# Joined inverses of two token tiles: turning four blocks of both tiles by one 128x128 transpose, with masks, sums and copies over two neighbouring banks

## The reference, cut to what matters

```python
A = jnp.where(strict, bc[..., :, None] * kk * decay, 0.0) + jnp.eye(C, dtype=jnp.float32)
u = lax.linalg.triangular_solve(A, bc[..., None] * vc, left_side=True, lower=True, unit_diagonal=True)
w = lax.linalg.triangular_solve(A, bc[..., None] * jnp.exp(G)[..., None] * kc,
                                left_side=True, lower=True, unit_diagonal=True)
```

```python
def step(state, inp):
    r_t, w_t, k_t, v_t, a_t, b_t = inp
    sa = jnp.einsum("bhvk,bhk->bhv", state, a_t)
    state = state * w_t[:, :, None, :] + sa[..., None] * b_t[:, :, None, :] + v_t[..., None] * k_t[:, :, None, :]
    return state, jnp.einsum("bhvk,bhk->bhv", state, r_t)
```

## Time and profile before

| | |
|---|---|
| three runs | 2663.7, 2663.72, 2672.25 us; median 2663.72 |
| profiled execution | 2665.42 us, its span 2663.6 us |
| PE matmuls | 2478.5 us busy (93%), 15332 |
| PE weight loads | 2084.5 us (78%), 15332 |
| DVE | 1805.8 us (68%), 2484 |
| ACT | 1426.0 us (54%), 1924 |
| POOL | 323.0 us (12%), 215 |
| mean granted TensorE clock | 0.948 |

### The profile page before, as it was taken

How to read it: one execution, slowest core, us unless ns; L and a number is a source line. 1 busy time by engine, 2 the same in 40 slices (tenths; PEclk the granted TensorE clock), 3 DMA queues, 4 the chain that set the end, 5 groups by cost and what they waited for, 6 DMA issues and landing times. The chain is left out here.

```text
span 2663.6 us, 40356 instructions
## 1 busy us (share of the span) xinstructions
PE 2478.5 (93%) x15332; PEld 2084.5 (78%) x15332; DVE 1805.8 (68%) x2484; ACT 1426.0 (54%) x1924; POOL 323.0 (12%) x215
## 2 busy tenths in 40 slices
PE   7878989998998999989998997799999999999998
PEld 6457658988886699866997986688888888888887
DVE  3665445557665555573455764788898888998897
ACT  4242234445553444243444642578777777778776
POOL 4110200004542000000002531000000000000000
PEclk9888799999999999988998999899999999999999
DMA  6510125543322255522554400899999999999995
GB/s 252 172 56 10 69 72 177 189 171 134 137 92 99 99 171 180 182 87 95 190 182 163 147 33 1 325 369 386 381 369 377 391 366 387 378 377 376 380 381 217
DMA packets 180012, 573.88 MB, mean 215 GB/s; under 512 B 11966, under 2 KB 81726, under 8 KB 136764
## 3 DMA queue, kind: packets, MB, share of 16 engines
q1 hardware_dynamic: 175932, 558.27, 56.3%
q0 software_dynamic: 2992, 11.01, 1.6%
q10 hardware_dynamic: 976, 3.03, 0.3%
HBM read 564.16 MB, written 6.29 MB: 214 GB/s over the span
## 5 line engine op out<-in xcount | busy, mean ns | idle before, releaser
L3637 DVE TENSOR_TENSOR moe_weights_low<-ring,moe_weights_high 128x1024 fp32r<-128x1024 f32 x672 | 779.8, 1218 | 95.5 <-ACT moe_weights_high L3886 95.4
L3886 ACT CAST moe_weights_high<-ring 128x1024 fp32r<-128x1024 f32 x672 | 687.0, 1053 | 108.9 <-PE banks L258 106.1
L256 PE MATMUL banks<-moe_weights_high,moe_rows_high 128*128 128x512 f32 x896 | 354.6, 396 | 3.1 <-DVE moe_rows_low L3642 2.5
L258 PE MATMUL banks<-moe_weights_low,moe_rows_high 128*128 128x512 f32 x896 | 350.2, 391 | 0.0
L257 PE MATMUL banks<-moe_weights_high,moe_rows_low 128*128 128x512 f32 x896 | 349.5, 390 | 0.0
L256 PE MATMUL banks<-ffn_x_high,ffn_weights_high 128*128 128x256 f32 x1056 | 299.1, 283 | 0.7 <-DVE ffn_x_low L3260 0.7
L257 PE MATMUL banks<-ffn_x_high,ring_low 128*128 128x256 f32 x1056 | 297.5, 282 | 0.0
L258 PE MATMUL banks<-ffn_x_low,ffn_weights_high 128*128 128x256 f32 x1056 | 297.4, 282 | 0.0
L3436 DVE TENSOR_TENSOR ring_low<-ring,ffn_weights_high 128x2048 fp32r<-128x2048 f32 x60 | 134.8, 2288 | 128.6 <-ACT ffn_weights_high L3410 128.6
L256 PEld LDWEIGHTS banks<-ffn_x_high,ffn_weights_high 128*128 128x128 f32 x1056 | 199.1, 189 | 4.2 <-DVE ffn_x_low L3260 1.4
L257 PEld LDWEIGHTS banks<-ffn_x_high,ring_low 128*128 128x128 f32 x1056 | 199.5, 189 | 2.7
(11 more groups left out here) (630 smaller groups left out, 4744.4 us busy)
## 6 DMA issues: line engine op xcount, KB each, us to landing
ring<-in_moe_gate_pieces SPq DMA_DIRECT2D x112, 1024.0 KB, 7.0
ring<-in_moe_up_pieces SPq DMA_DIRECT2D x112, 1024.0 KB, 7.2
ring<-in_moe_down_pieces SPq DMA_DIRECT2D x112, 1024.0 KB, 7.2
ring<-in_ffn_w SPq DMA_DIRECT2D x66, 1024.0 KB, 7.8
ring<-in_od_w_in SPq DMA_DIRECT2D x10, 2048.0 KB, 8.0
ring<-in_o_w_in SPq DMA_DIRECT2D x8, 2048.0 KB, 9.2
ring<-in_e_ffn_w_gate SPq DMA_DIRECT2D x11, 1024.0 KB, 5.4
ring<-in_e_ffn_w_up SPq DMA_DIRECT2D x11, 1024.0 KB, 8.0
```

Of the source, the lines that this page charges most:

```text
L256: pe.matmul(out_, lh, rh, start=start, stop=False)
L258: return pe.matmul(out_, lh, rl, start=False, stop=stop)
L3637: dve.tensor_tensor(lo[:, b], piece, hi[:, b].bitcast(F32), ALU.subtract).then_inc(sems["lo_done"], 1)
L3886: act.copy(hi[:, b * 1024:(b + 1) * 1024], piece).then_inc(sems["hi_done"], 1)
```

## The change

The two tiles of a pair now share one tile each for `blocks`, `blocks_t` and `low`. `blocks` is 128x512 with the columns ordered by head, tile, column, so that the 128 columns of one head hold both tiles' blocks side by side. T becomes one 128x128 transpose for each head (four a pair, into one bank), which puts the tile on the partitions and the side into the columns; one ACT copy of 128x512 takes it to `blocks_t`. P1 and P2 keep 16 products of 64x64: P1 writes with the tile on the partitions and one bank for each side, P2 takes tile on the partitions as input and writes side on the partitions, one bank for each tile. The mask, the sum and the first copy become single operations over two neighbouring banks, which a new helper `take_two` takes from an even number on, passing over a bank where the turn is odd. P1 and T of a pair are written in one go, each with its own semaphore count. `start_blocks` and `finish_inverse` read and write the new layout. An older function, `invert`, which nothing called, is removed.

```diff
+        def take_two():
+            if turn[0] % 2:
+                turn[0] += 1
+            at = turn[0] % BANKS
+            both_banks = psum[:, at * BANK:(at + 2) * BANK].rearrange("p (s n) -> p s n", s=2)[:, :, 0:256]
+            return [take_bank(), take_bank()], both_banks.rearrange("p s (j n) -> p s j n", j=4)
...
+                pair["by_tile"] = pair["blocks"].rearrange("p (j t n) -> p t j n", t=TT, n=64)
...
-                    for g, bank in zip(pair, two):
-                        act.copy(g["blocks"], bank.ap[:, 0:256]).then_inc(*S.tick())
+                    act.copy(pair["by_tile"], together).then_inc(*S.tick())
...
-                    two = [take_bank() for _ in pair]
+                    two, together = take_two()
+                    bank = take_bank()
...
                         for j in range(4):
-                            for g, bank in zip(pair, two):
-                                for b in sides:
-                                    last = pe.matmul(bank.ap[across(g, b), col(j)], g["NT"][b, j, b], g["blocks"][b, col(j)],
+                            for t, g in enumerate(pair["groups"]):
+                                for b, of_side in zip(sides, two):
+                                    last = pe.matmul(of_side.ap[sides[t], col(j)], g["NT"][b, j, b], pair["by_tile"][b, t, j, :],
                                                      start=True, stop=True)
                         last.then_inc(*M.tick())
-                    have = M.at()
+                        for due in unseen(pe, bank.free):
+                            pe.wait_ge(*due)
+                        for j in range(4):
+                            last = pe.transpose(bank.ap[:, j * P:(j + 1) * P], pair["blocks"][:, j * P:(j + 1) * P], ident)
+                        last.then_inc(*M.tick())
+                    turned = M.at()
+                    have = turned[0], turned[1] - 1
...
-                        for g, bank in zip(pair, two):
-                            dve.tensor_tensor(r4(g["low"]), r4(bank.ap[:, 0:256]), wide(const(f"level{s}")), ALU.mult).then_inc(*V.tick())
+                        dve.tensor_tensor(pair["low"].rearrange("p (j b n) -> p b j n", b=2, n=64), together,
+                                          const(f"level{s}").unsqueeze(1).unsqueeze(1).to_broadcast([P, 2, 4, 64]),
+                                          ALU.mult).then_inc(*V.tick())
...
-                        for j in range(4):
-                            for g, bank in zip(pair, two):
-                                for b in sides:
-                                    last = pe.matmul(bank.ap[across(g, b), col(j)], g["blocks"][b, col(j)], ident[b, b],
-                                                     start=True, stop=True)
...
-                        for g, bank in zip(pair, two):
-                            act.copy(g["blocks_t"], bank.ap[:, 0:256]).then_inc(*S.tick())
+                        act.copy(pair["blocks_t"], bank.ap.rearrange("p (s n) -> p s n", s=2)).then_inc(*S.tick())
...
                         for j in range(4):
-                            for g, bank in zip(pair, two):
-                                for b in sides:
-                                    there = across(g, b)
-                                    last = pe.matmul(bank.ap[b, col(j)], g["blocks_t"][there, col(j)], g["low"][there, col(j)],
+                            for t, of_tile in enumerate(two):
+                                for n_side, b in enumerate(sides):
+                                    at = 2 * j + n_side
+                                    last = pe.matmul(of_tile.ap[b, col(j)], pair["blocks_t"][sides[t], at // 4, col(at % 4)],
+                                                     pair["low"][sides[t], col(at)], start=True, stop=True)
...
-                        for g, bank in zip(pair, two):
-                            dve.tensor_tensor(g["blocks"], g["blocks"], bank.ap[:, 0:256], ALU.add).then_inc(*V.tick())
+                        dve.tensor_tensor(pair["by_tile"], pair["by_tile"], together, ALU.add).then_inc(*V.tick())
```

More of the change, by code:

```diff
@@ L1371, in _ @@
                         act.wait_ge(*turned)
-                        for g, bank in zip(pair, two):
-                            act.copy(g["blocks_t"], bank.ap[:, 0:256]).then_inc(*S.tick())
-                    for g, bank in zip(pair, two):
-                        bank.free = g["turned"] = S.at()
-                for n_pair, pair in enumerate(pairs):
-                    two = [take_bank() for _ in pair]
+                        act.copy(pair["blocks_t"], bank.ap.rearrange("p (s n) -> p s n", s=2)).then_inc(*S.tick())
@@ L1389, in _ @@
                         last.then_inc(*M.tick())
-                    have = M.at()
+                    have = pair["last_product"] = M.at()
                     @block.vector
                     def _(dve):
-                        for due in unseen(dve, [g["have"] for g in pair]):
+                        for due in unseen(dve, pair["have"]):
                             dve.wait_ge(*due)
                         dve.wait_ge(*have)
-                        for g, bank in zip(pair, two):
-                            dve.tensor_tensor(g["blocks"], g["blocks"], bank.ap[:, 0:256], ALU.add).then_inc(*V.tick())
@@ L1411, in _ @@
                 def _(pe):
-                    for due in unseen(pe, bank.free, bank2.free, g["have"]):
+                    for due in unseen(pe, bank.free, bank2.free, pair["have"]):
                         pe.wait_ge(*due)
                     for j in range(4):
-                        last = pe.matmul(bank2.ap[lower, col(j)], g["NT"][upper, j, lower], g["blocks"][upper, col(j)], start=True, stop=True)
+                        last = pe.matmul(bank2.ap[lower, col(j)], g["NT"][upper, j, lower], blocks[upper, j, :], start=True, stop=True)
                     last.then_inc(*M.tick())
@@ L1418, in _ @@
                         for b in sides:
-                            last = pe.matmul(bank.ap[b, col(j)], g["blocks"][b, col(j)], ident[b, b], start=True, stop=True)
+                            last = pe.matmul(bank.ap[b, col(j)], blocks[b, j, :], ident[b, b], start=True, stop=True)
                     last.then_inc(*M.tick())
@@ L1437, in finish_inverse @@
                 bank.free = g["turned"] = S.at()
-            for g in groups:
+            for pair in pairs:
+                g = pair["groups"][t]
+                low = pair["low"][:, t * 256:(t + 1) * 256]
                 bank = take_bank()
@@ L1445, in _ @@
                     for j in range(4):
-                        last = pe.matmul(bank.ap[upper, col(j)], g["low"][lower, col(j)], r4(g["XT"])[lower, j, lower], start=True, stop=True)
+                        last = pe.matmul(bank.ap[upper, col(j)], low[lower, col(j)], r4(g["XT"])[lower, j, lower], start=True, stop=True)
                     last.then_inc(*M.tick())
@@ L4708, in deltanet @@
             clear([*first, *second])
-            finish_inverse(first)
+            finish_inverse(pairs, 0)
             for w in first:
                 solve(w)
-            finish_inverse(second)
+            finish_inverse(pairs, 1)
             for w, w2 in zip(first, second):
```

222 lines of the change are left out of this document (36 added, 186 removed).

## The result

| | before | after |
|---|---|---|
| median, runs (lowest to highest) | 2663.70 us, 11 runs (2657.06 to 2672.25) | 2643.63 us, 11 runs (2641.31 to 2659.93) |
| a second set of runs | 2661.4 us, 23 runs (2653.08 to 2669.73) | 2643.73 us, 6 runs (2639.99 to 2653.02) |
| ratio of the times, 95% interval | | 0.9933 [0.9916, 0.995]; second set 0.9933 [0.9909, 0.9958] |
| profiled execution, span, granted clock | 2665.42, 2663.6, 0.948 | 2650.51, 2648.7, 0.952 |
| the same, a second profile | 2657.35, 2655.5, 0.953 | 2652.4, 2650.6, 0.95 |

The change makes the kernel faster, by 0.7% (0.4 to 0.9% by the two intervals). I had forecast 2652.8 us with a range that ended at 2646. The direction, the mechanism and the length of a level were right; the gain I gave was too small and the range too narrow.

The account below looks back on a forecast made before the run. TensorE's instruction fetch, 256 per 3.6 us, was taken to pace the inverses. Gains of 4.5 and 5.2 us there plus 1.2 in the finish, 10.9 together, took 2665.42 to 2654.5, or 2652.8 us as median; range 2646 to 2662.

Parts of the forecast that it names:

- The level: One of five levels of each inverse: 4.00 us by its path, 3.87 by the fetch, where it took 5.2.
- pair step: First product plus turn of one pair in a level: 1.20 us instead of 1.01, including 0.15 for the shape change.
- the way behind P2: From a level's second product to the next level: 1.66 us less 0.06 for the merged sum.
- The one stall: Fetch block arriving 0.4 us late at the first turn of the last level.
- the mask and the copy are covered: Within a level, mask ready at 1.57 us and copy of T at 1.90, before the second pair step ends at 2.40.
- The finish: Fetch stalls opening the finish of both inverses, 0.5 and 0.7 us, would go: 1.2 us gained.
- From the profiled execution to the median: Whole-run time: profiled forecast 2654.5 us, median taken 1.7 lower, 2652.8; 3 us added on either side for run spread.
- The first: Rival on the inverse's levels: the fetch keeps hold, 4.5 us a level, 2657.4 us on the median's scale; chance 0.14.
- the fourth: Rival on the inverse's levels: shape changes overlap with work, fetch paces levels at 3.87 us, median 2650.8 us; chance 0.10.
- The second: Rival on the inverse's stalls: not from instruction count, so they stay; levels 0.30 us longer, median 2666.7 us; chance 0.05.
- The third: Rival on TensorE's clock in the inverses: lower level granted, levels of 6.2 us, 2676.5 us; chance 0.05.
- The fifth: Rival on both stages: something beside the inverse sets their end, no change, median 2663.7 us; chance 0.04.

Follow-up runs that it names:

- e2: Changed kernel with merged masks, sums and copies kept, but the turn again by sixteen 64x64 products; 2658.9 us, 11 runs, ratio 0.9994 to the kernel before.
- e8: Changed kernel plus 14 idle small products (2 weight columns) per pair and level, 387 instructions a level as before the change; 2660.63 us, one run.
- e7: Changed kernel plus 35 small idle products (140 instructions) ahead of the first turn of mix0's inverse; first run 2640.84 us.
- e10: The same kernel as e7, timed: changed kernel plus 35 idle products ahead of mix0's first turn; 2644.3 us, ratio 0.9932 to the kernel before.

## Why the prediction was wrong, step by step

**What bounds the kernel: right.** Instructions arrived 256 at a time and paced the levels; e2 keeps the pace with the narrow turn, e8 brings it back by the count, and e7 moves the boundary.

**The level: right.** 4.00 us forecast; mix0's first products start at 218.52, 222.56, 226.57, 230.70 and 234.70, so 4.04, 4.01, 4.13 and 4.00. The pair step was 1.26 instead of 1.20 (0.20 between P1 and T where I had taken 0.15), and the way behind P2 1.57 instead of 1.60. The one stall stood at the turn that I had named and took 0.6 us and, in the second profile, 0.3, against 0.4. That the mask and the copy are covered held as well. In gdn the levels took 4.07, 4.36, 4.33 and 3.99 us, in the second profile 4.07, 4.36, 4.01 and 4.00. I had looked for one late block in each inverse; in gdn there was one in the second level and, in the first profile, another in the third. The second level took 4.36 us in e7 as well, whose block ended there without a pause; that one has a second cause, which stays open.

**The gain of the two inverses: right.** 9.7 us forecast. By the table the mean is 25.24 to 20.87 in mix0 and 26.11 to 21.06 in gdn, 4.4 + 5.0 = 9.4. It is the mean over two profiles that fits; the first pair alone gives 3.8 + 4.5.

**The finish: mis-sized.** I gave 1.2 us for two stalls that open it. From its first product to its last weight load it took 10.64, 9.43, 9.68 and 10.75 us before (mix0, gdn, then the second profile) and 8.38 or 8.44 after: 10.1 to 8.4, so 3.4 us for the two. The two without the lower clock (9.43, 9.68) give 1.0 and 1.3 each, twice what I took; the other two ran 5.0 and 3.4 us at the lower level. With the inverses this is 9.4 + 3.4 = 12.8; the remaining 0.4 of the 13.3 us lies in the first turn, which in one profile of after was spared the lower level. So the sum should have been 13.3 instead of 10.9.

**From the profiled execution to the median: this is the step that failed.** I took the median to lie 1.7 us below the profiled time, as it had in three runs, and allowed 3 us for the clock. Of the miss of 9.2 us, 6.8 lie here:
- 2.4 us are not of this step but of the finish and the first turn above.
- 2.8 us are the three runs of before: over 89 runs in five sets its median is 2660.9, not 2663.7.
- 4.0 us are left. The medians lie 2660.9 - 2643.6 = 17.3 apart, the stages 13.3. The runs of the kernel after fall into 13 from 2640.0 to 2647.0 us at mean granted clocks of 0.951 to 0.957, and 4 from 2650.5 to 2659.9 us at 0.948 to 0.952. Both profiled executions are among the four, so the traces show the rarer case, and the median leaves it out. The means, 2661.0 and 2645.8, lie 15.2 apart, with a standard error of 1.4.

So 13.3 us are accounted for in the traces. The rest of the kernel, the span less the two stages, shows what else moves the time: it took 2588.0 and 2577.7 us in the profiles of before, 2585.6 and 2586.7 in those of after, 2577.5 in e7 and 2576.8 in e10, where 262, 236, 256, 264, 235 and 233 us of it ran at the lower level. TensorE has the same instructions in it (the idle products of e7 and e10 apart), and its "issue" waits there were 9.6 to 10.9 us in all six. The kernel before reached a rest as short as e7's to 0.2 us, so no trace shows one that is shorter by the change. Whether the 2 to 4 us beyond the stages belong to the change (a lower level granted less often somewhere behind it) or to the chance of 17 runs is open; the wider interval of the ratio, 11 to 24 us, holds both.

**The rivals.** The first (4.5 a level) and the fourth (3.87, the change of shape for nothing) are both excluded by levels of 3.99 to 4.36, 4.10 on average. The second (stalls not from the number of instructions) is excluded by e7 and e8. The third looked for the lower clock inside the inverse; it was granted 1.00 there in both profiles, and it was the old inverse that ran 3.4 us of each at the lower level in both profiles. I had seen that on the earlier trace rows and weighed it only as a risk, not as something that could be gained back. The fifth is excluded by the result.

## What to carry to other kernels

Count the instructions of a small-tile loop, not only its products: where "issue" waits stand at equal distances in the count, one wide operation in place of many small ones paid here even though it is slower on the array, and making DVE and ACT lighter paid nothing until that was done. A wait of TensorE at such a place may be put down to another engine whose work had long ended. A gain read from one pair of profiles holds for the stage that was changed; before a difference elsewhere is put down to the change, profile the old kernel a second time. Where the granted clock differs by several thousandths from run to run, the range of a forecast has to be as wide as that makes it, whatever the sum says.

## What the runs showed of the hardware

- In these two loops TensorE got its instructions in blocks of 256, one in 3.58 to 4.10 us (e8), and paused up to 1.6 us at a boundary (before), in the middle of a group of like products.
- 140 idle instructions put into a wait ahead of mix0's inverse removed its last stall (0.6 us) altogether: where the boundaries fall decides it, and code that runs earlier sets that.
- In two executions of one program, the same stretch of small fp32 products took 47.61 and 39.58 us, at granted clocks of 0.56 and 0.73 with TensorE busy for 98 and 94% of it. 40 more products of 256 columns in it came with a shorter one (32.86 us at 0.93, one execution); 20 did not (39.07 us).
- Where 128x128 products follow 64x64 ones, their first load came 0.67 us after the first of 16 products of 64x64, where it was 0.47 with products of the same shape behind them (the order of those 16 differs too); on the way back 0.17 us passed without a load. Four such changes a level are in its 4.04 us.
